# Projections by spans of 512 tokens with half-block weight loads, and queries for 256 tokens at a time, in a hybrid decoder layer

## What is computed

```python
xn = rmsnorm(x, norm_gain)                       # x: 2048 prompt tokens, and 8 x 8 sample tokens; D = 1024
h = einsum('btd,dn->btn', xn, w_in)              # split: cb cc cu cz (512 each), q 512, k 128, v 128, az 512,
                                                 #        iq 512, ik 64, iw 8, gc 1024, ga 1024
y_conv = cb * conv3(cc * cu) * silu(cz)
# indexer: s[t, s'] = sum over 8 heads of iw * relu(iq . ik), causal; keep the best 256 keys of each token
# attention: 8 heads of 64, 2 kv heads, ALiBi, softmax over the kept keys; samples read a paged cache of 4096 keys
y_attn = attend(q, k, v, iq, iw, ik) * silu(az)
m = sigmoid(gc) * (y_conv @ w_up_conv) + sigmoid(ga) * (y_attn @ w_up_attn)
x = x + m @ w_out                                # then a last rmsnorm; k, v, ik and the conv state are outputs too
```

## Time and profile before

| | us |
|---|---|
| median of 3 runs | 2865.04 (2860.5 to 8133.02) |
| the profiled execution | 2864.7 |
| its span, first to last instruction | 2862.9 |
| TensorE busy | 2663.6 (93%) |
| VectorE busy | 1932.3 (67%) |
| ScalarE busy | 832.8 (29%) |
| mean granted TensorE clock | 0.974 of full |

### The profile page before, as it was taken

One profiled execution on the slowest core, in us unless ns is written; L12 is line 12 of the kernel. 1 busy time (PEld: TensorE's weight loads), 2 busy tenths in 40 slices (PEclk: granted clock), 3 DMA queues, 4 the chain that ended last, 5 costly groups with the idle time before them and its releaser, 6 DMA issues. The chain is left out here.

```text
span 2862.9 us, 31303 instructions
## 1 busy us (share of the span) xinstructions
PE 2663.6 (93%) x11650; PEld 1481.7 (52%) x11650; DVE 1932.3 (67%) x3938; ACT 832.8 (29%) x1363; POOL 49.0 (2%) x65
## 2 busy tenths in 40 slices
PE   7987998999999999999999998899999868999988
PEld 5743444454444545454545454555555546676653
DVE  5219899987797989887989997126995014454443
ACT  4222233322323233333333333311221342231210
POOL 0000000000000000000000000100000100000000
PEclk9998999999999999999999999899999989999999
DMA  7111111111111111111111010131225749453307
GB/s 213 32 37 35 43 42 41 31 46 35 40 45 35 36 38 30 41 38 37 33 35 35 26 43 24 52 115 72 103 104 126 220 193 292 156 187 108 129 30 30
DMA packets 212680, 215.33 MB, mean 75 GB/s; under 512 B 76720, under 2 KB 199216, under 8 KB 208880
## 3 DMA queue, kind: packets, MB, share of 16 engines
q1 hardware_dynamic: 203824, 153.13, 18.6%
q0 software_dynamic: 7072, 60.18, 6.8%
q10 hardware_dynamic: 1632, 0.01, 0.1%
HBM read 157.56 MB, written 55.72 MB: 74 GB/s over the span
## 5 line engine op out<-in xcount | busy, mean ns | idle before, releaser
L787 PE MATMUL attn_ps_r<-xnT,early 128*128 128x424 f32 (+2 forms) x2464 | 993.1, 543 | 30.5 <-ACT early L638 15.7
L115 DVE TENSOR_SCALAR_CACHE_REDUCE early<-early 128x384 uint8<-128x384 f32 (+13 forms) x462 | 681.8, 1476 | 11.5
L787 PEld LDWEIGHTS attn_ps_r<-xnT,early 128*128 128x128 f32 x2464 | 442.9, 191 | 441.0 <-issue 423.5
L1089 PE MATMUL samp_ps_r<-xnT,early 128*128 128x424 f32 (+1 forms) x800 | 288.2, 523 | 6.1 <-PEq L89 6.1
L657 ACT ACTIVATE attn_probT<-attn_ps_p 128x512 f32<-128x512 f32 (+1 forms) x288 | 151.9, 571 | 407.2 <-PE attn_ps_p L832 407.0
L1646 PE MATMUL merge_ps_y<-merge_w_out,merge_merged 128*128 128x512 f32 (+1 forms) x544 | 235.0, 592 | 1.2 <-DVE merge_merged L1775 1.2
L1089 PEld LDWEIGHTS samp_ps_r<-xnT,early 128*128 128x128 f32 x800 | 153.2, 192 | 138.9 <-issue 138.3
L715 DVE SCALAR_TENSOR_TENSOR early<-attn_relu,early 128x512 f32<-128x512 f32 (+3 forms) x266 | 182.1, 684 | 31.4 <-ACT attn_relu L674 4.1
L638 ACT ACTIVATE early<-attn_ps_r 128x424 f32<-128x424 f32 (+1 forms) x130 | 67.9, 523 | 427.8 <-PE attn_ps_r L787 426.5
L817 PE MATMUL attn_ps_s<-kT,qT 64*128 64x512 f32 (+3 forms) x640 | 163.9, 592 | 25.6 <-DVE early L744 18.5
L832 PE MATMUL attn_ps_p<-ident,prob 128*128 128x128 f32 x1088 | 156.8, 283 | 25.8 <-ACT prob L693 25.8
(11 more groups left out here) (231 smaller groups left out, 2366.0 us busy)
## 6 DMA issues: line engine op xcount, KB each, us to landing
rest_t<-early SPq DMA_DIRECT2D x144, 212.0 KB, 1.9
early<-in_w_in SPq DMA_DIRECT2D x104, 256.0 KB, 3.4
early<-in_x_prompt SPq DMA_DIRECT2D x16, 512.0 KB, 4.0
merge_x<-in_x_prompt SPq DMA_DIRECT2D x8, 1024.0 KB, 5.0
out_y_prompt<-merge_y POOLq DMA_DIRECT2D x16, 512.0 KB, 4.1
rest_t<-early SPq DMA_DIRECT2D x36, 208.0 KB, 2.1
merge_ga<-rest_t SPq DMA_DIRECT2D x7, 1024.0 KB, 10.9
merge_gc<-rest_t SPq DMA_DIRECT2D x7, 1024.0 KB, 9.4
```

The lines of the kernel that those rows point to most:

```text
L115: self.v.done(self.nc.vector.tensor_scalar(self.hits, self.x, limit, None, op, ALU.add, accum_out=self.count))
L787: ins = nc.tensor.matmul(ps_r[:, 0:width], w_rest[:, n % 2, k, :], c.xnT[:, k, t0:t0 + width], start=(k == 0), stop=(k == KC - 1))
L1089: ins = nc.tensor.matmul(ps_r[:, i % 2, 0:width], w_rest[:, (slot0 + j) % 2, k, :], c.xnT[:, k, t0:t0 + width], start=(k == 0), stop=(k == ...
```

## The change

- The sample tokens come first in `xnT` (columns 0 to 63), the prompt behind them.
- Queries: `stage_norm` makes the indexer's for the samples alone and attention's for 64 + 256 tokens in one matmul per step. The others are made in the attention stage for `QB` = 256 tokens at a time, two indexer and two attention items in each T.
- The rest: each of the 36 blocks is projected for the samples and the first 512 tokens as two items of 288 (`whole`), in T = 2 to 9. For the three other spans of 512 tokens a `group` of two blocks is four items of 256 tokens (`part`), 54 groups in all, 34 of them in T = 10 to 16 and 20 in the sample stage. A block's weights are thus loaded four times.
- Weights: a load is half a block (four of eight chunks of channels), as two DMAs, into a ring of eight. From group 20 on (`FAR`) four of the slots and the results lie in the columns of `xnT` that span 1 has left free; before that in a new tensor `more`.
- The plan gives out whole items only.
- Sample stage: SP, which loads and stores the rest, also stores the bias and issues the replicas, behind the last store; POOL's keys(2) waits for the last stores of the rest; ScalarE does exp(0) and exp(1) behind all copies.

```diff
+QB = 256
+SPAN = 512
+HALF = SPAN // 2
-REST_LOADS = [0, 0, 0, 1, 1, 1, 1, 2, 2, 2, 2, 2, 3, 3, 3, 3, 0]
+BLOCKS = 4 * len(GROUPS)
+NPAIR = BLOCKS // 2
+NGROUP = NPAIR * (NPASS - 1)
+PART = (ST + SPAN) // 2
+RING = 8
+FAR = NPAIR + 2
+PAIRS_OF_TILE = [0, 0, 1, 2, 2, 2, 2, 3, 3, 3, 0, 0, 0, 0, 0, 0, 0, 0]
+GROUPS_OF_TILE = [0, 0, 0, 0, 0, 0, 0, 0, 0, 0, 4, 5, 6, 6, 6, 5, 2, 0]
+def slot_of(c, load, group=0):
...
+    n = load % RING
+    if n < 4:
+        return c.w_near[:, n]
+    return c.xnT[:, 0:4, ST + SPAN + (n - 4) * P:ST + SPAN + (n - 3) * P] if group >= FAR else c.w_more[:, n - 4]
+def weight_pieces(a, block, half, dst):
...
+    return [(dst[:, 2 * n:2 * n + 2], win[:, 2 * n:2 * n + 2, col:col + P]) for n in range(2)]
...
@@ stage_norm, TensorE
-                    if g >= 4:
-                        pe.wait_ge(q_kept, g - 3)
...
                     for k in range(KC):
-                        last = nc.tensor.matmul(ps_q[:, g % 4, t0:BAND], w[:, k, :], c.xnT[:, k, t0:BAND],
-                                                start=(k == 0), stop=(k == KC - 1))
+                        if g < 4:
+                            last = nc.tensor.matmul(ps_kv[:, 0, g * ST:(g + 1) * ST], w[:, k, :], c.xsT[:, k, :],
+                                                    start=(k == 0), stop=(k == KC - 1))
+                        else:
+                            last = nc.tensor.matmul(ps_q[:, g - 4, 0:ST + QB], w[:, k, :], c.xnT[:, k, 0:ST + QB],
+                                                    start=(k == 0), stop=(k == KC - 1))
-                    for k in range(KC):
-                        last = nc.tensor.matmul(ps_kv[:, 0, g * ST:(g + 1) * ST], w[:, k, :], c.xsT[:, k, :],
-                                                start=(k == 0), stop=(k == KC - 1))
@@ AttentionPlan
+                for i in (2 * (t % TPQ), 2 * (t % TPQ) + 1) if 0 <= t < NT and h < NQ else ():
+                    items.append(Item(kind, h, i, len(self.loads), KC))
+                    self.loads += [(kind, h, i, half) for half in range(2)]
+            for pair in range(pair, pair + PAIRS_OF_TILE[T]):
+                for n in range(4):
+                    items.append(Item("whole", 2 * pair + n // 2, n % 2, len(self.loads) + n // 2 * 2, KC))
+                self.loads += [("block", 0, 2 * pair + n // 2, n % 2) for n in range(4)]
+            for group in range(group, group + GROUPS_OF_TILE[T]):
+                items += [Item("part", group, n, len(self.loads) + n // 2 * 2, KC) for n in range(4)]
+                self.loads += [("part", group, n // 2, n % 2) for n in range(4)]
@@ shares
-        total = len(self.items[T]) * KC
-        edges = [round(total * sum(wide[:n]) / sum(wide)) for n in range(len(wide) + 1)]
-        return [edges[n + 1] - edges[n] for n in range(len(wide))]
+        for n in range(len(wide)):
+            end += wide[n] / sum(wide) * total
+            count = 0
+            while sum(fill) + count < len(items) and done + items[sum(fill) + count].steps / 2 <= end:
+                done += items[sum(fill) + count].steps
+                count += 1
+            fill.append(count)
+        fill[-1] += len(items) - sum(fill)
+    def split(self, count, ahead=False):
...
+        early = 1 if ahead and count > 1 else 0
+        first = (count - early + 1) // 2
+        return early, first, count - early - first
@@ prompt attention, SP
+                        for l in plan.free[n]:
+                            sp.wait_ge(rest_done, n + 1)
+                            load(l + RING)
...
+                        if item.kind == "part" and item.i == 3:
+                            sp.wait_ge(rest_kept, n + 1)
+                            store_group(item.of)
@@ prompt attention, TensorE
+                            if n:
+                                pe.wait_ge(rest_kept, n)
+                            for k in range(item.steps):
+                                load = item.load + k // 4
+                                if k % 4 == 0:
+                                    pe.wait_ge(w_in[load % RING], 32 * (load // RING + 1))
...
@@ sample stage, SP
+                for n in range(in_all):
+                    sp.wait_ge(rest_done, n + 1)
+                    if n % 2:
+                        load(n - 1 + RING)
+                        load(n + RING)
+                    if n >= 4 and n % 4 == 0:
+                        store_group(GROUP0 + n // 4 - 1)
+                store_group(NGROUP - 1)
                 for s in range(2):
+                    sp.wait_ge(rest_stored[s], 32 * sum(g % 2 == s for g in groups))
...
                 sp.wait_ge(biased, 1)
+                sp.dma_start(a["bias_scratch"].rearrange("b t k -> (b t) k"), score[0:ST, :]).then_inc(bias_out, 16)
+                sp.wait_ge(bias_out, 16)
+                replicate(0)
+                replicate(1)
+                sp.wait_ge(added, 1)
+                replicate(2)
+                sp.wait_ge(added, 2)
+                replicate(3)
@@ sample stage, POOL
-                pool.wait_ge(biased, 1)
-                pool.dma_start(a["bias_scratch"].rearrange("b t k -> (b t) k"), score[0:ST, :]).then_inc(bias_out, 16)
-                pool.wait_ge(bias_out, 16)
-                replicate(0)
-                replicate(1)
-                pool.wait_ge(rest_done, len(steps))
+                pool.wait_ge(rest_done, in_all)
+                for s in range(2):
+                    pool.wait_ge(rest_stored[s], 32 * sum(g % 2 == s for g in groups))
                 keys(2)
                 values(1)
@@ sample stage, TensorE's order and ScalarE's
-        RESTS = [NCH * n for n in (2, 3, 6, len(loads) - 1, len(loads))]
+        RESTS = [GROUP0 + n for n in (4, 6, 12)] + [NGROUP]
...
                 exp(0)
-                keep_rest(RESTS[3], RESTS[3] + 2)
                 exp(1)
-                keep_rest(RESTS[3] + 2, RESTS[4])
                 keep_probs(0)
```

More of the change, by code:

```diff
@@ L479, in __init__ @@
         self.weighs0 = before([G * len(x) for x in self.subs])
-        self.stores0 = before([sum(load[0] == "rest" for _, load, _ in x) for x in self.items])
         self.fill = [self.shares(T) for T in tiles]
@@ L681, in _ @@
                         for ch in range(before):
[L682 removed]
+                            early, first, second = fill.slot(g > 0 and ch == 0)
                             keep_rest(early)
```

382 lines of the change are left out of this document (200 added, 182 removed).

## The result

The changed kernel takes 3054.28 us (median of 4 runs, 3051.11 to 3058.16) where the kernel before took 2863.7 beside it: a ratio of 1.067, with a 95% interval of 1.0649 to 1.0691. One of the kernel before's four executions took 8133 us; the ratio is taken without it. The prediction was 2883 us with a range of 2842 to 2930. It was wrong by 171 us, and outside its range. The profiled execution has a span of 3052.3 us, 189.4 more than the kernel before.

The account below looks back on a forecast made before the run. TensorE was taken to bound most tiles, VectorE tile 15. Norm -32, attention +32, samples -6 and sample-stage end +25 gave +19 us on a median of 2865.04: 2883 us, range 2842 to 2930.

Parts of the forecast that it names:

- The norm stage's end: End of norm stage: indexer queries for samples alone, attention's for 64 + 256 columns together; -32 us.
- the samples until the last projection: Sample stage up to its last projection: 282.1 us of matmul records become 276.5; -6 us.
- rival D: Projection matmuls: each of 2240 more records pays an exposed 191 ns weight load; +428 us, 3311 us; chance 0.01.
- Weights were late: Weight loads from DRAM: forecast 0; as a rival, sample-stage gathers stall the ring, +30 us, 2913 us; chance 0.05.
- the floor of tile 15: Attention stage, tile 15: loses 16 us of TensorE work but falls only to VectorE's floor, about 153 us; +14 us.
- Tile 2 took its work for nothing: Attention stage, tile 2: gets 15.6 us of work and has 14 us of TensorE idle; -14 us.
- Coarser filling: Attention stage: 3.5 us pieces cannot be shared over short slots, mostly absorbed by two-deep ps_s; +4 us (-5 to +25).
- Fragments: Attention stage: 228 stretches of projection in place of 338, 110 fewer at 0.15 us per end; -16 us (-11 to -31).
- One bank: Attention stage: items in a row wait for ScalarE's copy from ps_r; +11 us; as a rival +72, 2944 us, chance 0.12.
- the columns: Attention stage: projection records cost 942.3 us after against 898.6 before, from the sum of columns; +43.7 us.
- The tail: End of sample stage: bias store and replicas start only after the last projection, 149 us against 124; +25 us (+5 to +35).
- Rival A: Attention stage and sample end: unbroken items run better, filling costs nothing, replicas pass gathers unhindered; 2845 us; chance 0.14.

Follow-up runs that it names:

- single steps: Changed kernel with projections handed out by single steps (eight per item) over the attention stage's slots, as the kernel before cuts them: 2958.3 us, ratio 1.0328.
- the cover: Changed kernel plus four 256-column matmuls, results unread, ahead of each pair's transposes where no item stands (48 places): 3029.2 us, ratio 1.0585.

## Why the prediction was wrong

**Right.** The norm stage's end (-32 forecast, -32.4 measured) and the samples until the last projection (-6, -5). 256-column records start 216 ns apart (64 in 13.98 us), so rival D is out. Here the trace goes against the Trainium skill's sentence (TensorE: Matmul & The Clock Gate, section The mechanism), by which a load overlaps matmuls only when its row group differs: loads of the full array, 190 to 196 ns each, stood between them. Weights were late only at the stage's start (6.0 us). VectorE is the floor of tile 15: with single steps the tile takes 154.0 us, as before, though TensorE is busy for 136.0 us of it in place of 147.1. Tile 2 took its work for nothing. In the run with single steps tiles 8 and 9 are 9.9 and 9.6 us shorter, as worked out (10 each), tile 7 only 4.3, and tile 11 is 14.4 longer (12).

**The step that failed** is "Coarser filling: +4 us (-5 to +25)". It measured 98 us (stretch of tiles 2 to 16, whole against single steps). I had asked whether a 3.5 us piece fits into a slot, which I took ps_s with its two entries to absorb, and not on which side of the waiting instruction it stands. The two entries absorbed it only in part: the indexer's waits for their copies went from 10.9 to 30.1 us. The larger part is the waits for Exp, 77.5 us more. At 48 of 64 starts of a pair nothing stood ahead of the transposes: at 25 because `split` puts a slot's only item behind them, so that TensorE waited out Exp with the item in hand, and at 23 because `shares` gave the slot no item. Both functions were in the code that I read. And the price of a gap was not the gap alone: 70 of the 98 us were idle time, the other 28 busy time of the same records, beside 85.3 us more at half clock (129.7 for 44.4).

**Fragments** were forecast at -16 us: fewer ends between projection and other work. The busy time of the projections after is 85 us over their columns (1027.6 for 942.3), where it was 94.5 before, so -9 with the lower clock in it, and the gain was worth far less than what it was bought with.

**One bank** (+11) measured -4 in the kernel after (18.0 for 22.2 us). With single steps it is +22 (43.9 us, 89 waits). With the columns (+43.7) that is more than the 62.5 us by which the attention stretch of that kernel is longer than before. Tiles 2 and 16 go the other way: their idle time falls from 26.0 to 7.5 us, as the forecast had it, while tile 15's rises from 7.2 to 18.0, VectorE's floor. Tiles 12 and 14 grew by 15 and 18 us where 4 each were forecast; the bank explains 4 and 3 us of it (5.8 for 1.4 us of waits in tile 12, 3.8 for 0.7 in tile 14), and the rest was not taken apart.

**The tail** had the right mechanism and the right place, and one term of the wrong size: "15 until the first replica is added, 10 until the second". I took both from the earlier trace rows, where the replicas went over POOL's queue, for a kernel that sends them over SP's. Measured there: 36.4 and 25.4. The upper bound, +35 "if they share", was too low, since sharing was only one of two causes. On the terms' own queue the sum comes out within a microsecond (149.6 for 149), partly by luck: the bias store took 10.7 us there, not 8, and the first replica 17.4, not 15, and the 5 us set aside for sharing made up for them.

**The chances.** The two misses, 133 us in the attention stage and 35 in the tail, are 168 of the 171. Slower by over 2% had 0.15, mostly for a rival (one bank) that turned out false; the true one was in the sum, at +4. Rival A's replicas that pass the gathers nearly unhindered (17.4 us) were seen only on POOL's queue, issued ahead of them.

**Open.** Half clock and waiting were separated only by the cover, which changes both at each place. How the 30 us of waits for the indexer's copies would move the clock alone was not tried. Why a replica on SP's queue goes out eight packets at a time, and on POOL's 16, is not shown; no run here has the same replicas in other shapes.

## What to carry to other kernels

Work that fills an engine's waits is worth its place, not its amount: put it ahead of the instruction that waits, in pieces small enough that each wait gets one, and check a coarser schedule by how many waits are left bare. Give a moved transfer the duration of the queue that it moves to; a row of the old queue doesn't price it. A move of work out of a stage where it stood bare (here 32 us of queries) is paid in the stage where it lands, at that stage's rate, so look first at tiles whose engine is idle and at half clock, where a block of 28 us cost 11.

## What was not expected of the hardware

- Gaps of 1 to 2 us of TensorE can be followed by half clock: 5.88 us for an item that took 3.72 just ahead of the gap. Not each is: behind one of 1.38 us, at 1825.27 in the changed kernel, an item took 3.62. 83 us of added matmuls in such gaps (76 in tiles 2 to 16) made the kernel 25 us faster, with half clock in those tiles down from 129.7 to 34.1 us.
- The replicas of the first pair (two transfers of 1040 KB, with the second pair's two behind them) took 22.3 us on SP's queue at a DMA share of 0.49, eight packets at a time, with no gathers beside them, and 17.4 us on POOL's queue, mostly 16 packets at a time, with gathers behind them.
- On SP's queue, behind and beside 8 MB of gathers, the same took 36.4 us; ordered ahead of them on POOL's queue it was 17.4, for 14.7 before with no gathers beside them.
